# Head 0's third and fourth combination moved ahead, and one memory area placed before the normalized input

## What is computed

```python
p = u @ od_w_in[j]                       # u = rms_norm(x, norm_pre[i])
q, k, v, r, lr = jnp.split(p, [...], axis=-1)
g = log_sigmoid(lr @ w_gate_up + b_gate) / 16
# chunks of 64 tokens; S is the running state of a head
attn = where(causal, (qi * exp(bi)) @ (ki * exp(-bi)).T, 0)
o = attn @ vi + (qi * exp(bi)) @ S
y = (rms_norm(o, norm_g) * silu(r)) @ od_w_out[j]
```

## Time and profile before

| | |
|---|---|
| median of three runs | 1596.4 us (1595.74 to 1596.65) |
| the profiled execution, its own time | 1596.45 us |
| its span (first to last instruction) | 1594.7 us |
| granted TensorE clock, mean | 0.998 of full |
| PE busy | 1577.0 us (99%) |
| DVE busy | 1163.5 us (73%) |
| ACT busy | 730.1 us (46%) |
| matrix instructions | 8985 |

### The profile page before, as it was taken

The page is one execution under the profiler, slowest core; times in us unless marked ns, Lnnn a source line. Parts: engine busy times, 40 slices in busy tenths (PEclk is TensorE's granted clock), DMA queues, the critical chain, the costliest instruction groups (busy, mean ns, idle before and its releaser), DMA issues.

```text
span 1594.7 us, 22200 instructions
## 1 busy us (share of the span) xinstructions
PE 1577.0 (99%) x8985; PEld 1374.2 (86%) x8985; DVE 1163.5 (73%) x1542; ACT 730.1 (46%) x996; POOL 206.4 (13%) x241
## 2 busy tenths in 40 slices
PE   9999999999999999999999999999999899999998
PEld 7888888888998999888998889878888788988887
DVE  5267274667888898556999999984475868677677
ACT  5333242253541355345454554568255436455364
POOL 4991000000000000004223221122010000000000
PEclk9999999999999999999999999999999999999999
DMA  8664633231342333524978897698533123322241
GB/s 246 171 176 127 163 119 107 66 106 53 107 132 80 106 107 106 196 81 175 251 155 214 187 202 190 135 208 184 174 120 93 31 90 107 104 72 79 66 159 67
DMA packets 166635, 211.84 MB, mean 133 GB/s; under 512 B 52177, under 2 KB 102021, under 8 KB 165894
## 3 DMA queue, kind: packets, MB, share of 16 engines
q1 hardware_dynamic: 146725, 176.31, 35.6%
q0 software_dynamic: 18144, 31.99, 11.6%
q10 hardware_dynamic: 1664, 2.13, 0.5%
HBM read 193.63 MB, written 16.78 MB: 132 GB/s over the span
## 4 chain that ended last, share of the span: by engine, by line
PE 92%; DVE 3%; DMA 2%; ACT 2%; issue 0%; SPq 0%; DVEq 0%; ACTq 0%
PE PS L2988 58%; PE PS L3192 20%; PE PS L2966 3%; PE PS L3410 1%; PE PS L3065 1%; DMA WR<-in_ev_w_in_dram 1%; PE PS L3342 1%; PE PS L3244 1%; PE PS L3440 1%; PE PS L3175 1%; DMA WL<-in_ev_w_in_dram 1%; PE PS L3158 0%; PE PS L3416 0%; PE PS L3270 0%; PE PS L3143 0%
## 5 line engine op out<-in xcount | busy, mean ns | idle before, releaser
L1148 ACT ACTIVATE WH<-WR 128x1024 fp32r<-128x1024 f32 x160 | 169.6, 1061 | 419.0 <-PE PS L2988 366.5
L2988 PE MATMUL PS<-HH,WH 128*128 128x512 f32 x800 | 312.1, 390 | 0.8 <-ACT G L1237 0.4
L2988 PE MATMUL PS<-HL,WH 128*128 128x512 f32 x800 | 311.4, 389 | 0.0
L2988 PE MATMUL PS<-HH,WL 128*128 128x512 f32 x800 | 311.3, 389 | 0.0
L1821 DVE TENSOR_TENSOR WL<-WR,WH 128x1024 fp32r<-128x1024 f32 x104 | 138.4, 1339 | 219.0 <-ACT WH L1148 218.5
L1162 ACT ACTIVATE WHS<-WRS 128x1024 fp32r<-128x1024 f32 x112 | 117.6, 1057 | 179.0 <-PE PS L2988 71.4
L2988 PEld LDWEIGHTS PS<-HH,WH 128*128 128x128 f32 x800 | 150.2, 188 | 33.7 <-issue 2.1
L2988 PEld LDWEIGHTS PS<-HH,WL 128*128 128x128 f32 x800 | 150.2, 188 | 31.3
L2988 PEld LDWEIGHTS PS<-HL,WH 128*128 128x128 f32 x800 | 150.2, 188 | 30.8
L1830 DVE TENSOR_TENSOR WLS<-WRS,WHS 128x1024 fp32r<-128x1024 f32 x112 | 136.6, 1221 | 49.5 <-ACT WHS L1162 49.1
L2459 DVE SCALAR_TENSOR_TENSOR TMP<-CP,PRM,TMP 128x512 f32<-128x512 f32 x232 | 154.9, 741 | 0.0
(11 more groups left out here) (540 smaller groups left out, 3431.1 us busy)
## 6 DMA issues: line engine op xcount, KB each, us to landing
WR<-in_w_in_dram SPq DMA_DIRECT2D x56, 512.0 KB, 4.3
WRS<-in_w_in_dram SPq DMA_DIRECT2D x40, 512.0 KB, 4.2
WR<-in_ev_w_in_dram SPq DMA_DIRECT2D x24, 512.0 KB, 5.0
WL<-in_ev_w_in_dram POOLq DMA_DIRECT2D x24, 512.0 KB, 8.0
WRS<-in_od_w_in_dram SPq DMA_DIRECT2D x24, 512.0 KB, 4.2
WR<-in_od_w_in_dram SPq DMA_DIRECT2D x20, 512.0 KB, 4.2
WR<-in_ev_w_in_dram SPq DMA_DIRECT2D x32, 256.0 KB, 3.2
WR<-in_ev_w_out_dram SPq DMA_DIRECT2D x16, 512.0 KB, 4.8
```

Of the source, the lines that this page charges most:

```text
L1148: act.activation(WH[:, n % RING, :, :], WR[:, n % RING, :, :], ACT.Copy).then_inc(w_hi, 1)
L2988: mm = pe.matmul(out_banks[m], st, mv, start=(kt == 0 and i == 0), stop=(kt == 2 * per - 1 and i == 2))
```

## The change

Three of the edits are in the code of head 0. On DVE `combine_rest` now follows `combine_first` directly, before the gates; the low parts of `S1` and `S2` follow the split of the first three chunks of `r.0`; the low parts of `G3` and `G4` take the place where `combine_rest` was. On ACT the high parts of `G3` and `G4` follow the split of the same three chunks, before the copy of `qk.0`. No instruction is added or taken away, and PE, SP and POOL keep their order.

The fourth edit moves `R1` in the list of areas from behind `YL` to behind `WL`. With the start of the list counted as 0, `HH` moves from 49152 to 66496, `HL` from 65536 to 82880, `YH` from 81920 to 99264, `YL` from 98304 to 115648, and `R1` from 114688 to 49152. The areas from `R2` on stay where they are, and so do `WR`, `WH`, `WL`. 17344 is no multiple of 1024: the four halves now start 960 bytes behind one.

```diff
-        for name, size in (("WR", 16384), ("WH", 16384), ("WL", 16384), ("HH", 16384), ("HL", 16384),
-                           ("YH", 16384), ("YL", 16384), ("R1", 17344), ("R2", 16384), ("R3", 16384),
+        for name, size in (("WR", 16384), ("WH", 16384), ("WL", 16384), ("R1", 17344), ("HH", 16384),
+                           ("HL", 16384), ("YH", 16384), ("YL", 16384), ("R2", 16384), ("R3", 16384),
...
                 if first:
                     whole_high(r, range(3))
+                    head_combination_hi(3, [x[:, :, 0:SEQ // 2] for x in G3H], [x[:, :, 0:SEQ // 2] for x in G3R])
+                    head_combination_hi(4, [G4H[:, :, :]], [G4R[:, :, :]])
                     qk_out(op_end("qk.0"), A)
...
                 whole_high(r, range(3, 4))
-                if first:
-                    head_combination_hi(3, [x[:, :, 0:SEQ // 2] for x in G3H], [x[:, :, 0:SEQ // 2] for x in G3R])
-                    head_combination_hi(4, [G4H[:, :, :]], [G4R[:, :, :]])
-                else:
+                if not first:
...
                     combine_first()
+                    combine_rest()
...
                 if first:
                     whole_low(r, range(3))
+                    head_combination_lo(1, [S1L[:, :, :]], [S1R[:, :, :]], [S1H[:, :, :]])
+                    head_combination_lo(2, [S2L[:, :, :]], [S2R[:, :, :]], [S2H[:, :, :]])
...
                 if first:
                     whole_low(r, range(3, 4))
-                    combine_rest()
-                    head_combination_lo(1, [S1L[:, :, :]], [S1R[:, :, :]], [S1H[:, :, :]])
-                    head_combination_lo(2, [S2L[:, :, :]], [S2R[:, :, :]], [S2H[:, :, :]])
+                    head_combination_lo(3, [x[:, :, 0:SEQ // 2] for x in G3L], [x[:, :, 0:SEQ // 2] for x in G3R], [x[:, :, 0:SEQ // 2] for x in G3H])
+                    head_combination_lo(4, [G4L[:, :, :]], [G4R[:, :, :]], [G4H[:, :, :]])
...
                 next_low(qk, 3)
-                if first:
-                    head_combination_lo(3, [x[:, :, 0:SEQ // 2] for x in G3L], [x[:, :, 0:SEQ // 2] for x in G3R], [x[:, :, 0:SEQ // 2] for x in G3H])
-                    head_combination_lo(4, [G4L[:, :, :]], [G4R[:, :, :]], [G4H[:, :, :]])
                 inner(qk)
```

## The result

| kernel | median us | runs | ratio to before | span us |
|---|---|---|---|---|
| before | 1596.53 | 4 (1595.74 to 1596.82) | 1 | 1594.7 |
| changed | 1610.9 | 4 (1610.32 to 1611.1) | 1.009 (95%: 1.0074 to 1.0106) | 1609.1 |

The account below looks back on a forecast made before the run. PE was taken to bound the kernel, standing in 92% of the chain that ended last. From 1596.45 us, -8.9 for head 0's wait and clock and -0.4 for the memory area gave 1587.1, range 1575.5 to 1592.

Parts of the forecast that it names:

- The wait and the clock: Head 0, first score to first block product: PE's 6.58 us wait and the half-clock stretch both go, 13.65 to 4.71, -8.9 us.
- the exchange between ACT and DVE: Head 0, weights of qk.1 ahead of the SiLU: DVE's first low part at 1242.5, the exchange ending at 1249.3.
- the margin of 0.5: Head 0, ACT's SiLU: it waits for the end of r.0 anyway, with 0.5 us to spare.
- a wait that shrinks and stays: Head 0: DVE or ACT fall behind, PE stands again 1 to 3 us, 1589 to 1592 us; chance 0.06.
- The area: Moved areas: -10.3 us on block products, +10.4 on ordinary ones, -0.5 on output products, -0.4 us in all.
- all ordinary products: 4524 products between the weights and HH, HL, YH, YL: 2.3 ns more each, +10.4 us.
- block products on `H` and `G4`: 1536 instructions on HH, HL and G4 gain 6.7 ns each at 960 bytes behind, -10.3 us.
- output products: Heads' output products, OH and OL now both 960 behind: 288 instructions, up to 2 ns less each, -0.5 us.
- the pool row: 48 pool products, weights 960 behind a multiple of 1024 and YH not: 229.0 ns each, 2.3 ns more than HH against WH.
- the ordinary products pay more: At L2988, reads of weights and moving data meet oftener; from 4.4 ns each it outweighs all gains, 1607 at 6.7; chance 0.07.
- Only the gain comes: Block products take the quick pace, ordinary ones keep theirs: 1576.7 us; chance 0.25.
- Place plays no part: The 7 ns between block products come from something else S1, S2, S4 share; only the -8.9 us counts: 1587.5 us; chance 0.22.

Follow-up runs that it names:

- the first experiment: The changed code with the old list of areas, against the kernel before: 1587.85 us, ratio 0.9948.

## Why the prediction was wrong

**The wait and the clock: right.** 13.65 us became 4.71, no stretch of head 0 is at 0.50, and the code alone brought -8.8 us where -8.9 was worked out. The steps held too. The order of the exchange between ACT and DVE was no longer what the SiLU waits for; ACT stood 0.48 us before it, about the margin of 0.5 that had been worked out. DVE's first low part of the weights, put at 1242.5, starts at 1242.81 in the first experiment:

```profile
1242.81 1.22 DVE L1829 TENSOR_TENSOR WLS<-WRS,WHS 128x1024 fp32r<-128x1024 f32 x1
```

No new wait came behind the attention. The rival of a wait that shrinks and stays is refuted by the missing row for `RR`.

**The area: -0.4 us forecast, +23.1 measured.** That place plays a part was right, and so was the idea that the distance to the weights is what counts; the experiments with `R1` in front and with 64 bytes behind it showed that. Wrong were the sizes. Worked out from the starts of all matmuls in the traces of the first experiment and of the changed kernel, whose spans differ by 1609.1 - 1586.2 = 22.9 us (the forecast priced 4524 ordinary products, and 4416 of them are in the first three rows; the rest are at most 0.3 us at its 2.3 ns):

| term | forecast us | measured us |
|---|---|---|
| ordinary products, `H` moving, 2400 | | +15.2 |
| ordinary products, `Y` moving, 960 | | +5.9 |
| ordinary products, `H` stationary, 1056 | | +3.2 |
| all ordinary products | +10.4 | +24.3 |
| block products on `H` and `G4` | -10.3 | -4.4 |
| products on `S1`, `S2`, `S4` | none | +3.0 |
| output products | -0.5 | +0.7 |
| all else | none | -0.9 |
| sum | -0.4 | +22.7 |

**The step that failed** is "I take 2.3 ns because the pool row is the same shape at the same distance, though with moving and stationary operand exchanged; the block products, where both directions can be seen, do not care for the direction". In both the input moves and the weights stand; what is exchanged is which of the two lies 960 bytes behind. So the pool pair is at +64 and the new pairs of the moving halves at -64, and at 512 columns these differ: 2.3 against 6.5 ns, as the kernel with 64 bytes before `HH` showed by giving 229.1 at +64. Even at +64 the 2.3 ns was no safe price: the pool products themselves paid 6.6 in the kernel with `YH` and `YL` before `R1`. The block products were no witness for the 512-column shape, since for them distance 0 is the slow case. The average over all ordinary products came to 24.3 / 4416 = 5.5 ns, beyond the 4.4 from which the rival on the slower side was said to decide. That rival, **the ordinary products pay more**, named the right line, and its 1607 at 6.7 ns was 4 us short of the time; its chance, 0.07, was too small. What was said against it, that no product at a single distance is that slow, is true of before, but no steady stretch of 512-column products at -64 stands there to be read (the pool products and those of `W` moving against `OL` are at +64; only a few of the attention, between shorter ones, are at -64). So the case that covers 3360 instructions, the halves moving at -64, was unseen.

**The block products** were to gain 6.7 ns on 1536 instructions and gained 4.4 us in all. With weights moving they went from 119.9 to 114.8, most of the forecast 6.7; with `HH` moving only from 119.8 to 117.6. The timeline of PE in the changed kernel shows why the mean is in between. In head 0, behind the attention, first the steps over the change from `HH` to `S1`, then further down over that from `G4` to `HH`:

```profile
1280.15 0.28 PE L3190 MATMUL PS<-HH,WLS 128*128 128x256 f32 x1
1280.26 0.28 PE L3190 MATMUL PS<-HH,WHS 128*128 128x256 f32 x1
1280.37 0.28 PE L3190 MATMUL PS<-HL,WHS 128*128 128x256 f32 x1
1280.49 0.28 PE L3190 MATMUL PS<-HH,WLS 128*128 128x256 f32 x1
1280.60 0.28 PE L3190 MATMUL PS<-S1H,WHS 128*128 128x256 f32 x1
1280.71 0.28 PE L3190 MATMUL PS<-S1L,WHS 128*128 128x256 f32 x1
...
1281.85 0.28 PE L3190 MATMUL PS<-S1H,WLS 128*128 128x256 f32 x1
```

```profile
1302.25 0.28 PE L3190 MATMUL PS<-G4H,WHS 128*128 128x256 f32 x1
...
1302.96 0.28 PE L3190 MATMUL PS<-HH,WHS 128*128 128x256 f32 x1
...
1303.90 0.28 PE L3190 MATMUL PS<-HH,WLS 128*128 128x256 f32 x1
```

From 1280.15 to 1281.85 there are 15 steps, 113.3 ns each; from 1302.25 to 1303.90 there are 14, 117.9 each. Operands at one distance run at two paces, and in both places the pace goes on across the change of operand. So the pace of a pair is not set by its own distance alone. Before the change `HH` at 0 and `S1` at -64 stood beside each other at 119.8 and 114.1; with both at -64 they take 117.6 and 117.3. That is the +3.0 us of the unmoved `S`, a term that the forecast put at nothing. In the kernel with `YH` and `YL` before `R1` it is there too (`S1` 116.8), so it goes with the place of `HH` and `HL`, and not with that of `Y`. What chooses between the paces was not found.

**Only the gain comes** fell with 233.3 ns. **Place plays no part** fell with the 17.9 us that 64 unused bytes are worth. The Trainium skill ("TensorE: Matmul & The Clock Gate", section "Step-by-step: what each phase is for") says that the next weights' loading takes no read bandwidth from the running matmul; the rival drew on that, and the times don't bear the conclusion out. The runs don't show that reads collide; they show that the pace of a matmul depends on where its two operands lie to each other.

## What to carry to other kernels

Before moving a memory area whose size isn't a multiple of 1024, list the start distance of each moving operand to its weights before and after: here distance 0 was best for 512-column products and worst for 256-column ones, and 64 bytes at one place in the list were worth 17.9 us of 1611. A row may price an edit only if its shape and its distance, with the sign, agree; where one differs, the range has to reach to the bound on the bad side. Even where they agree the price held in most stretches, not in all. And when an edit joins a reordering with a layout, the two are measured apart: the gain of 8.8 us was hidden by a loss of 23.

## What was not expected of the hardware

- 128x512 products of this kernel start 226.7 ns apart where moving operand and weights start a multiple of 1024 bytes apart, 233.3 at -64 and +32, 233.0 at +128, and 228.9 or 233.3 at +64. Distances between 128 and 512 bytes were not tried.
- At 256 columns the order is the reverse: 119.8 to 120.2 ns in the mean at 0, and 114.1 to 118.8 at the other distances of the table.
- At 512 columns no difference was seen by which operand moves. The one section whose weights are read in strides of four took 0.31 us for a load and 235.0 ns from start to start at distance 0, where the others took 0.19 and 226.7; that the stride is the reason was not tested.
- Open: the mechanism; what chooses between 228.9 and 233.3 ns at +64 and between 113.3 and 118 at 256 columns; and why +64 can be milder than +32 and +128.
